# The end of a hybrid encoder block: the last four down steps bank by bank, and the last four output tiles normalised in halves on two engines

## The reference, cut to what matters

```
def rms_norm(x, gain):
    y = xf * lax.rsqrt(jnp.mean(xf * xf, axis=-1, keepdims=True) + RMS_EPS)
    return (y * gain)
...
    h = rms_norm(x, norm_ffn[l])
    x = x + (jax.nn.gelu(gate) * val) @ w_down[l]      # val, gate: conv of h @ w_up[l]
return rms_norm(x, norm_final)
```

## Time and profile before

| | us |
|---|---|
| median of 3 runs | 2441.06 |
| lowest and highest run | 2440.95, 2443.32 |
| the profiled execution | 2442.07 |
| its span, from first to last instruction or transfer | 2440.3 |

### The profile page before, as it was taken

One profiled execution on the slowest core, in us unless ns is written; L12 is line 12 of the kernel. 1 busy time (PEld: TensorE's weight loads), 2 busy tenths in 40 slices (PEclk: granted clock), 3 DMA queues, 4 the chain that ended last, 5 costly groups with the idle time before them and its releaser, 6 DMA issues.

```text
span 2440.3 us, 33112 instructions
## 1 busy us (share of the span) xinstructions
PE 2394.8 (98%) x11450; PEld 1962.8 (80%) x11450; DVE 1726.8 (71%) x2569; ACT 747.5 (31%) x1431; POOL 846.3 (35%) x689
## 2 busy tenths in 40 slices
PE   7999999999999999999999999999999999999997
PEld 6887778887888888878888777888878888888886
DVE  6965555637999999989750345465478888888896
ACT  4145114213333333332222441142233333333222
POOL 2422223531555555523233222236113333333221
PEclk9999999999999999999999999999999999999999
DMA  6276553441343444598522545435212222217963
GB/s 209 67 189 151 173 167 123 152 167 61 129 139 128 133 142 149 210 372 285 178 98 79 127 118 187 149 123 196 99 58 89 86 77 77 95 66 267 347 222 138
DMA packets 178278, 367.33 MB, mean 151 GB/s; under 512 B 22344, under 2 KB 60008, under 8 KB 178168
## 3 DMA queue, kind: packets, MB, share of 16 engines
q1 hardware_dynamic: 135568, 278.23, 34.7%
q10 hardware_dynamic: 42600, 87.64, 10.5%
HBM read 277.20 MB, written 88.60 MB: 150 GB/s over the span
## 4 chain that ended last, share of the span: by engine, by line
PE 92%; DVE 3%; DMA 2%; ACT 1%; issue 1%; SPq 0%; POOL 0%; DVEq 0%; ACTq 0%; POOLq 0%
PE ps L497 29%; PE ps L499 29%; PE ps L498 29%; PE ps L2239 1%; PE ps L2241 1%; PE ps L2221 1%; PE ps L2042 1%; PE ps L2178 1%; PE ps L2189 1%; PE ps L2169 1%; DMA ff<-z 1%; PE ps L2092 0%; DVE act_lo L1853 0%; DMA step_w<-tw 0%; DMA gates<-junk 0%
## 5 line engine op out<-in xcount | busy, mean ns | idle before, releaser
L844 POOL CAST slot_hi<-pair_raw 128x512 fp32r<-128x512 f32 x220 | 197.3, 904 | 399.3 <-PE ps L499 310.6
L497 PE MATMUL ps<-act_hi,w_hi 128*128 128x512 f32 x832 | 330.7, 398 | 0.0
L499 PE MATMUL ps<-act_hi,w_lo 128*128 128x512 f32 x832 | 324.5, 390 | 0.0
L498 PE MATMUL ps<-act_lo,w_hi 128*128 128x512 f32 x832 | 323.9, 389 | 0.0
L798 POOL CAST w_hi<-w_raw 128x1024 fp32r<-128x1024 f32 x72 | 77.2, 1073 | 647.4 <-PE ps L499 622.7
L497 PE MATMUL ps<-act_hi,slot_hi 128*128 128x512 f32 x704 | 274.3, 390 | 1.8 <-DVE pre L1806 1.5
L499 PE MATMUL ps<-act_hi,slot_lo 128*128 128x512 f32 x704 | 273.9, 389 | 0.0
L498 PE MATMUL ps<-act_lo,slot_hi 128*128 128x512 f32 x704 | 273.9, 389 | 0.0
L497 PE MATMUL ps<-act_hi 128*128 128x512 f32 x616 | 241.8, 392 | 5.7 <-DVE act_lo L1857 5.7
L499 PE MATMUL ps<-act_hi,act_lo 128*128 128x512 f32 x616 | 240.7, 391 | 0.0
L498 PE MATMUL ps<-act_lo,act_hi 128*128 128x512 f32 x616 | 240.7, 391 | 0.0
(11 more groups left out here) (320 smaller groups left out, 4876.3 us busy)
## 6 DMA issues: line engine op xcount, KB each, us to landing
w_raw<-in_wu SPq DMA_DIRECT2D x88, 512.0 KB, 3.6
pair_raw<-in_wu SPq DMA_DIRECT2D x88, 512.0 KB, 3.9
step_f<-ff SPq DMA_DIRECT2D x88, 512.0 KB, 5.2
ff<-z SPq DMA_DIRECT2D x44, 512.0 KB, 2.6
gates<-junk ACTq DMA_DIRECT2D x64, 256.0 KB, 2.1
sig<-gates ACTq DMA_DIRECT2D x32, 512.0 KB, 5.4
tbl_o<-tables ACTq DMA_DIRECT2D x32, 384.0 KB, 3.6
step_w<-in_wu SPq DMA_DIRECT2D x22, 512.0 KB, 6.5
```

The source lines that it names most:

```text
L497: nc.tensor.matmul(out, lh, rh, start=first, stop=False, skip_group_check=onto)
L498: nc.tensor.matmul(out, lh, rl, start=False, stop=False, skip_group_check=onto)
L499: return nc.tensor.matmul(out, ll, rh, start=False, stop=last, skip_group_check=onto)
L844: nc.gpsimd.tensor_copy(slot_hi[j][:, :, :], src).then_inc(slot_half[KIND[j]], 1)
```

## The change

In pass 3 of block 1 the last four steps instead of two are run bank by bank (`chunk`). In ACT's program four squares are added behind `value_hi` of steps 39 to 42: the right halves of tiles 4 to 7, summed into a new `stat_late["ssq"]`. On DVE, behind the scaling of tiles 0 to 3, there is now the right half's part of the variance for all four tiles at once, and then four multiplications of the right halves by the gain. After that DVE goes tile by tile: add the bank, wait for the sum of squares of the left half, finish the variance, wait for the root, make the reciprocal, signal it, scale the left half. ACT, for each tile, squares the left half, takes the root, scales the right half by the reciprocal, waits for its own result and for the left half, and issues the store. The diff, with unchanged lines left out:

```
+        stat_late = {n: keep(f"{n}_late", [TT]) for n in ("ssq", "var")}
...
+        def chunk(blk, p):
+
+            return 2 * CHUNK if p == PASSES - 1 and blk + 1 == BLOCKS else CHUNK
...
             def square(src, stat, i, sq, count):
 
                 wait(act, sq, count - 1)
-                nc.scalar.activation(junk[i % 2][:, :].bitcast(BF16), src, ACT.Square,
+                nc.scalar.activation(junk[i % 2][:, :].bitcast(BF16)[:, 0:src.shape[-1]], src, ACT.Square,
                                      accum_out=stat["ssq"][:, i:i + 1]).then_inc(sq, 1)
...  (ACT, in the loop over steps, behind value_hi(t))
                     if 35 <= t < 39:
                         out_square(blk, t - 35)
+                    if blk + 1 == BLOCKS and 39 <= t < 43:
+                        square(xres[:, HK + t - 39, HALF:], stat_late, HK + t - 39, sq_o, blk * TT + t - 35)
                     if t == 39:
                         root(stat_o, var_o, std_o, out_parts(blk), 0, 4)
...  (ACT, block 1, behind the loop)
                     for i in range(4, TT):
-                        out_square(blk, i)
+                        act.wait_ge(dn_evac, tile_count(blk, i))
+                        square(xres[:, i, 0:HALF], stat_o, i, sq_o, blk * TT + HK + i)
                         root(stat_o, var_o, std_o, out_parts(blk) + i - 3, i, i + 1)
-                        if i > 4:
-                            store_out(blk, i - 1)
-                    store_out(blk, TT - 1)
+                        act.wait_ge(o_ready, blk * TT + HK + 2 * (i - HK) + 1)
+                        order.mark(copy(xres[:, i, HALF:], xres[:, i, HALF:], scale=stat_o["rstd"][:, i:i + 1]))
+                        order.settle(act)
+                        act.wait_ge(o_ready, blk * TT + HK + 2 * (i - HK) + 2)
+                        act.dma_start(A["out"].rearrange("(n p) d -> n p d", p=P)[blk * TT + i], xres[:, i, :]).then_inc(out_st, 16)
...  (DVE, behind out_scaled(0) to out_scaled(3))
-                for q in range(HK if blk + 1 == BLOCKS else 0):
-                    bank_add(24 + q)
-                    if q:
-                        out_norm(blk, HK + q - 1, HK + q, out_parts(blk) + q)
                 if blk + 1 == BLOCKS:
-                    out_norm(blk, TT - 1, TT, out_parts(blk) + 4)
+                    late = slice(HK, TT)
+                    dve.wait_ge(sq_o, blk * TT + TT)
+                    order.mark(v.tensor_scalar(stat_late["var"][:, late], stat_late["ssq"][:, late], 1.0 / D, EPS, ALU.mult, ALU.add))
+                    for i in range(HK, TT):
+                        ins = tt(xres[:, i, HALF:], xres[:, i, HALF:], gfin[:, HALF:], ALU.mult)
+                    order.mark(ins)
+                    order.settle(dve)
+                    for i in range(HK, TT):
+                        c = slice(i, i + 1)
+                        bank_add(20 + i)
+                        dve.wait_ge(sq_o, blk * TT + HK + i + 1)
+                        order.mark(stt(stat_o["var"][:, c], stat_o["ssq"][:, c], 1.0 / D, stat_late["var"][:, c], ALU.mult, ALU.add))
+                        order.settle(dve)
+                        dve.sem_inc(var_o, 1)
+                        norm_rstd(stat_o, i, i + 1, std_o, out_parts(blk) + i - HK + 1)
+                        dve.sem_inc(o_ready, 1)
+                        stt(xres[:, i, 0:HALF], xres[:, i, 0:HALF], stat_o["rstd"][:, c], gfin[:, 0:HALF], ALU.mult, ALU.mult).then_inc(o_ready, 1)
...  (PE, in the loop over steps: `some` stands for CHUNK)
+                    some = chunk(blk, p)
-                    if t % PAIRS_K < PAIRS_K - CHUNK:
+                    if t % PAIRS_K < PAIRS_K - some:
...
-                        for m in range(t, t + CHUNK):
+                        for m in range(t, t + some):
                             pe.wait_ge(step_ready, operands_by(blk, m))
                         for q in range(HK):
                             for n in range(products(t)):
                                 end = q == HK - 1 and n == products(t) - 1
-                                for m in range(t, t + CHUNK):
-                                    ins = down_bank(m, n, q, False, m == t + CHUNK - 1)
-                                    if end and m < t + CHUNK - 1:
+                                for m in range(t, t + some):
+                                    ins = down_bank(m, n, q, False, m == t + some - 1)
+                                    if end and m < t + some - 1:
                                         ins.then_inc(d_used, 1)
```

More of the change, by code:

```diff
@@ L2409, in _ @@
                             next_transposed(blk + 1, t - X_STEP)
-                    elif t % PAIRS_K == PAIRS_K - CHUNK:
-                        for m in range(t, t + CHUNK):
+                    elif t % PAIRS_K == PAIRS_K - some:
+                        for m in range(t, t + some):
                             pe.wait_ge(step_ready, operands_by(blk, m))
```

## The result

The changed kernel takes 2444.38 us (median of 22 runs, 2443.62 to 2446.77), the kernel before 2440.99 in the same runs (22, 2440.08 to 2443.32): a ratio of 1.0014 with a 95% interval of 1.0008 to 1.0020. It is 3.4 us slower, within the 0.2% that counts as no change, and the interval leaves out 1. The forecast was 2444.3.

What follows compares the result with a forecast made beforehand. PE, 98% busy, bounds the kernel until its last matmul, then DVE's instruction list. +2.55 ahead of the first bank, +1.05 for three cycles, -0.33 for the last tile: +3.27 on 2441.06, so 2444.3 us; range 2442.3 to 2446.9.

Steps and rivals of the forecast that it cites:

- PE's pause: PE, ahead of step 40: waits 2.2 us for step 43's operands, costing nothing, with 7 us of slack.
- The early squares: ACT, behind high parts of steps 39 to 42: some 0.8 us each, first delays step 40's low parts, costing nothing.
- The work ahead of the first bank: DVE, before bank 24's add: a small operation and four multiplications move that add from 2423.35 to 2425.9, +2.55 us.
- The cycle: DVE and ACT, per tile: DVE stands still for ACT's half square, 3.59 us from add to add instead of 3.24.
- The last tile: Last of the four tiles: add at 2436.7, store issued at 2440.46 instead of 2437.19; its own term -0.33 us.
- The sum: Whole tail: +2.55 ahead of the first bank, +1.05 for three cycles, -0.33 for the last tile: +3.27 us, median 2444.3.
- The share: ACT instead of DVE scaling the right half: gains 0.6 us in each cycle and 0.5 on the last tile.
- ACT's queue: Rival: next square stands behind this tile's store on ACT, slack 0.08 us; +5.6 us, 2446.7; chance 0.09.
- The clock: Rival: granted clock falls in PE's wait ahead of step 40; +7.0 us, 2448.1, or hidden; chance 0.05.
- The third rival: Rival: scaling of tiles 0 to 3 and early weighting cost nothing, last bank sets end: -3.8 us, 2437.3; chance 0.04.

Runs made afterwards that it cites:

- three steps alone: Kernel before with the last three steps bank by bank instead of two, all else as before: 2440.87 us, ratio 1.0000.
- the kernel without the share: Changed kernel with DVE scaling the right half too, ACT only squaring, taking the root and issuing the store: 2446.16 us, ratio 1.0018.
- the overlap put back: Changed kernel with DVE adding the next tile's bank ahead of this tile's variance, ACT squaring the next tile before scaling: 2441.58 us, ratio 1.0000.
- the first form of the parts together: Three steps bank by bank, scaling of tiles 0 to 2 between steps 40 to 43, tiles 4 to 7 in two pairs: 2439.86 us, 0.9995 of before.
- PE's part alone: Kernel before with only the last four steps bank by bank, nothing on ACT or DVE, profiled three times: 2441.05 us, ratio 0.9998.
- the second form of the parts together: Three steps bank by bank, right-half multiplications of tiles 4 to 6 behind operands of steps 40 to 42, tiles in pairs: 2437.94 us, 0.9988 of before.
- PE's part undone: Changed kernel with the last two steps bank by bank, as before, instead of four: 2444.50 us, ratio 1.0012.
- three steps: Changed kernel with the last three steps bank by bank instead of four: 2444.81 us, ratio 1.0016.
- the scaling moved: Changed kernel with scaling of tiles 0 to 2 moved behind the operands of steps 40 to 42 on DVE: 2442.99 us, ratio 1.0008.

## Why the prediction was right

**PE's pause.** Forecast 2.2 us, from 2416.3 to 2418.5, the clock kept, seven microseconds of slack. Measured 2.16, the last matmul at 13.24 behind step 39, DVE's last add at 20.39, so 7.1 of slack; undoing PE's part left the tail where it was. Right, and shown.

**The early squares.** Forecast 0.8 us on the operands of step 40, covered. In the changed kernel DVE's last low part of step 40 ends at 2410.85 instead of 2410.52, and that of step 43 ends 1.97 behind step 39 as before. The size was too large; that it costs nothing was right.

**The work ahead of the first bank.** Forecast +2.55, the first add at 2425.9, 9.4 behind step 39. Measured +2.41, at 9.27. The multiplications start 0.60 apart, as the adds did, and moving them into the gap gave 2.52 back.

**The cycle.** Forecast 3.59, measured 3.70 to 3.72. The terms of the first tile: square start behind the add 0.72, variance 0.75 behind the square's start (forecast 0.81: the row it was taken from, 1.24 for a whole tile, has DVE busy with bank 25's add; in three steps alone, where DVE waits for the square, it is 1.18), reciprocal 0.49 (0.47), last small operation 0.77 (0.78), scaling 0.32 (0.21), next add 0.67 (0.60). The two terms that were too small are the signal between the reciprocal and the scaling, and the half scaling: it takes 0.75, not 0.68, with ACT's scaling beside it or, in the kernel without the share, without. The mechanism, that DVE stands still while ACT squares the same tile, is shown by the 0.79 in each cycle and by the overlap put back.

**The last tile.** Forecast 24.0 behind step 39 for the last store, measured 24.26. ACT's half took 0.72, as taken from between two rows.

**The sum.** +3.27 forecast; +3.56 in the profiled execution's tail (24.26 less 20.70) and +3.39 in the medians. By terms, forecast and tail: +2.55 and +2.41 ahead of the first bank, +1.05 and +1.40 for three cycles, -0.33 and -0.25 for the last tile. The first error hides part of the other two, and that the median came out within 0.1 us of 2444.3 is in part luck: the same sum misses the tail by 0.3. One reading of the range was off: the runs of before do not lie within 1 us of their middle, one of the three was 2.26 above it. Nothing hung on that.

**The share.** Here a term was mis-sized: 0.6 in each cycle and 0.5 on the last tile were said to be gained by ACT's half; the run without it shows 0.29 in a cycle and 1.09 in all. I had priced DVE's right half by the two-operand row; the form with one operand takes 0.41 to the next start, and the signal to ACT that it saves is 0.12. The sum did not rest on it. The Trainium skill's rule against multiplying on ScalarE (ScalarE: Activation LUTs, Rules for kernel authors) holds per instruction, 0.72 on ACT against 0.49 on DVE (the 0.62 to 0.81 against 0.68 of the prediction had left it open), and by the path ACT's half still gains, 0.29 in a cycle, though half of what was said.

**The rivals.** ACT's queue kept a slack of 0.1 us, as thin as the forecast's 0.08: the next square started at 2430.13, 0.71 behind its add as the first tile's did with no store ahead of it (0.72), and 0.54 behind the start of the store's issue, where ACT needed 0.44. It bound in the overlap put back and in the first form of the parts together. The clock did not fall in the pause of the changed kernel's profiled execution but did in one of three executions of PE's part alone, with the same pause; I had put it down as unlikely because 2.2 us was short of the 4.1 after which it fell before. That argument failed: in that execution it fell 2.7 us after the last matmul, and 4.1 is one value of many, as the last section shows. Had it fallen so in the changed kernel, PE would have ended 1.6 us later, inside the slack of 7.1; in that execution DVE added bank 25 at 9.51 behind step 39, and the changed kernel asks for it only at 12.99. That this leaves the time alone is still argued and not shown. The third rival's gain of 3.8 did not come, for the reason given against it: the first bank's add moved 2.41 later. A version with DVE's list in another order, the second form of the parts together, is 2.9 below before.

## What to carry to other kernels

Work that is put earlier on an engine gains nothing if it stands in the same list ahead of the work that everyone waits for: ask for each moved instruction which idle time it now fills, and put it there (a wait for another engine, a gap between operands). Going tile by tile undoes an overlap when another engine's result for this tile has to be awaited on the spot: with one tile of distance put back, the cycle here went from 3.70 to 2.83. And before a producer is reordered to finish its parts earlier, check when the consumer first asks: here bank 24 was ready some 4.2 us before it was wanted (2429.67 less 36 matmuls of 0.227, against 2425.70).

## What the runs showed of the hardware

- The granted clock can fall in a pause of 2.16 us: it did in one of seven profiled executions with that pause, 2.7 us after PE's last matmul and 0.6 us after its restart, for about 3.4 us. It fell in the one with a pause of 3.14 us, and in this stretch in none of the six with a pause of 0.42 us or none (before, PE's part undone, three steps, three steps alone, both forms of the parts together). The Trainium skill (TensorE: Matmul & The Clock Gate, HAM oscillation) ties the fall to waits between groups of matmuls; the runs agree, and show that one and the same pause may cost the clock or not.
- Behind the last matmul of all, the granted clock fell to 0.50 in each of the fourteen profiled executions, but 1.95 us after that matmul's end in one (overlap put back: 2428.60 to 2430.55) and up to 5.3 us after it in others (the changed kernel, the scaling moved, the second execution of PE's part alone). So a pause is not safe because it is shorter than the 4.1 of the earlier trace rows. PE's last matmul in the overlap put back, and the window in which the clock fell:

```profile
2428.21 0.39 PE L504 MATMUL ps<-act_hi,act_lo 128*128 128x512 f32 x1
```

```profile
2430.00:2432.00 2.00, 0.00 (x0) 0.00 (x0) 1.72 (x5) 0.72 (x2) 0.00 (x0) 0.64 0.30 121
```

- With the scaling moved, two scalings of 128x1024 on DVE beside a POOL copy of a 128x512 tile took 1.66 and 1.63 us instead of 1.28, the copies 0.61 and 0.65; beside the first moved scaling it was the copy that took longer, 1.50 us instead of 0.61, and the scaling took its 1.28.
- In the second form of the parts together two stores of 512 KB issued within 0.85 us end 4.51 us behind the last issue; in the changed kernel, where they are 3.70 apart, the last one ends 3.11 behind its own.
